# The gating stage of a PEER feed-forward block: distances by TensorE from bf16 digits, digit products by GpSimd, every fourth one-hot by VectorE, and the end of the routing moved into the down pass

## The chip, the cores and the metric

The kernel runs on one core of one Trainium2 chip. The metric is the device time of one execution in microseconds (us), here the median of three runs. One execution is profiled as well; its span and its own time are given below.

## What is computed

The reference is two blocks in sequence, on 256 tokens of 1024 values (16 meta tokens are put ahead of them). The first has a state-space mixer with a convolution branch and a PEER feed-forward; the second has two layers with attention and two SwiGLU feed-forwards each. Only the PEER part matters here:

```python
v1, i1 = lax.top_k(s1, 16); v2, i2 = lax.top_k(s2, 16)      # 8 heads, 128 keys in each half
cand = v1[..., :, None] + v2[..., None, :]
cand_idx = i1[..., :, None] * 128 + i2[..., None, :]
top_s, pos = lax.top_k(cand, 16); expert_idx = take(cand_idx, pos)
gate = jax.nn.softmax(top_s, axis=-1)
act = gelu(einsum("td,thkd->thk", xb, w_down[ib])) * gb
y = einsum("thk,thkd->td", act, w_up[ib])
```

So each token has 128 slots (8 heads by 16), each slot an expert of 16384 (its first key, 0 to 127, and its second key, 0 to 127) and a gate.

## The kernel before, in words

The kernel gathers nothing. The **down pass** computes the hidden value of all 16384 experts for all 256 tokens: 128 units of weights (one unit is 128x1024 values, 512 KB, and makes the hidden values of the 128 experts of one first key, one row of `hid`), each loaded by SyncE into one of 4 slots of `ring`, split by ScalarE (`w_hi`, L415) and VectorE (`ring_lo`, L421) into two fp32r parts, and multiplied by TensorE in 24 matmuls of 256 columns (L526 to L528). ScalarE then applies Gelu from one of PSUM's banks 0 to 3 into `hid` (L2037). `loop_8` is TensorE's side of it, `hidden` ScalarE's, the `low("down", ...)` calls VectorE's. ScalarE and VectorE work two units ahead of TensorE.

Beside the first three quarters of the down pass VectorE does the top-k. Its last part is short: softmax over the slots (ScalarE's Exp at L2043, which in this kernel stands after unit 112, `SAFE` = 28 turns of 4 units; VectorE's sum, reciprocal and product, L1530 to L1532, after the pass), and a split of the second key into a low digit (its value modulo 8, `exp_low`) and a high one (`exp_high`, a multiple of 8).

The **routing's end** comes after the down pass. TensorE transposes first keys, high digits, gates and low digits (L796, banks 4 and 5), so that slots lie on the partitions and tokens along the free axis. VectorE copies three of them to `slot_t` (L1535, L1536), and makes the table `gate_low` in banks 0 to 3 (L1540, L1542; 256 tokens by 8: the gate where the low digit matches, else 0) and the table `high_digit` for 128 tokens by 16 (L1546; 1 where the high digit matches), which it makes again for the second 128 tokens.

The **gating** turns slots into a dense gate per expert and token. It goes in 32 groups n of 8 tokens, with two buffers of each kind. For each group:
- GpSimd writes `diff`, index minus first key, 128x1024 (L2315);
- ScalarE makes of it the one-hot `hots` (`hot_a` in the code): Abs (L2058), then Relu of 1 minus that (L2060), the second in place;
- VectorE writes the digit product `hot_keys` (`hot_b`): high digit by low digit and gate, 128x1024 (L1558);
- TensorE multiplies the two, token by token: 8 fp32 matmuls of 128x128 by 128 columns (L806), which the trace shows as 16 instructions each of weight load and matmul, into banks 4 and 5 or 6 and 7;
- VectorE multiplies the result into `hid` (`big` in the trace, L1565).

The order on each engine is that of its instructions; the semaphores `gates_mm`, `hot_abs`, `hot_diff`, `hot_act`, `hot_dve` and `gated_hid` join them. When the last group is done, the **up pass** starts: ScalarE and VectorE split `hid` (L2050, L1585) and the weights, and TensorE multiplies (L827, 12 matmuls of 512 columns in a unit, 128 units). SyncE has loaded its first four units ahead of the gating, then waits for `gates_mm` 32, issues the loads of `h` (L477, L479), and only then goes on with the stream. ScalarE's queue issues the copy of a bias table within the chip's memory (`bias_rows` from `u_table`, L2062), which the second block needs, just ahead of the gating.

## Time and profile before

| | |
|---|---|
| median of 3 runs | 2464.0 us (2463.56 to 2464.43) |
| profiled execution | 2459.27 us, of which the span from the first to the last instruction is 2457.4 us |
| TensorE matmul busy | 2268.8 us, 92% of the span |
| VectorE busy | 1666.1 us, 68% |
| ScalarE busy | 1140.0 us, 46% |
| GpSimd busy | 250.9 us, 10% |
| mean granted TensorE clock | 0.957 of full |

The profile is of one execution. PE is TensorE's matmul, PEld its weight load, which overlaps PE, DVE is VectorE, ACT ScalarE, POOL GpSimd, SP SyncE; a small q behind a name is that engine's sequencer. Times count from the first instruction. A row names the line, the tiles written and read, the shape, and the number of instructions; what stands in brackets is the engine's idle time before, with what ended it. A matmul's own duration (for 128 columns some 0.27) has its way through the array in it: matmuls follow each other faster than that, so their pace is read from a count over a stretch.

### The profile page before, as it was taken

How to read it: one execution, taken by the hardware profiler on the slowest of the kernel's cores; microseconds unless marked ns; L12 is line 12 of the kernel's file. 1: busy time of each engine (PE TensorE's matmuls, PEld its weight loads, DVE VectorE, ACT ScalarE, POOL GpSimd, SP SyncE). 2: the span in 40 equal slices, each digit the busy share in tenths (PEclk: the TensorE clock that was granted, in tenths of full speed). 3: DMA queues.
4: the chain of work that ended last, by engine and by line, in shares of the span. 5: the costliest groups of instructions: out<-in, count | busy, mean ns of one | idle time of the engine just before them, and what ended most of it. 6: DMA issues, size and time to landing. Idle time of an engine off the chain costs nothing.

```text
span 2457.4 us, 43049 instructions
## 1 busy us (share of the span) xinstructions
PE 2268.8 (92%) x15536; PEld 2077.4 (85%) x15536; DVE 1666.1 (68%) x2997; ACT 1140.0 (46%) x1615; POOL 250.9 (10%) x159
## 2 busy tenths in 40 slices
PE   6988899999988999999799997699999999679999
PEld 5987799999977788888799986499999996457999
DVE  6799569989759655555776644377667665844774
ACT  4432247777768555555444433343444342233443
POOL 4751100000017100000210100010010010001000
PEclk8998999999989999999899997699999998989999
DMA  4432455665560466666555541055555562202655
GB/s 135 148 98 85 129 164 183 185 187 182 186 207 0 143 188 188 188 188 190 171 171 177 175 128 43 9 162 171 175 185 172 170 195 71 69 1 86 188 180 180
DMA packets 107969, 359.47 MB, mean 146 GB/s; under 512 B 12992, under 2 KB 21568, under 8 KB 107760
## 3 DMA queue, kind: packets, MB, share of 16 engines
q1 hardware_dynamic: 105792, 354.04, 46.8%
q10 hardware_dynamic: 2096, 4.36, 0.5%
q8 instruction: 50, 0.82, 0.1%
q14 instruction: 31, 0.25, 0.0%
HBM read 356.22 MB, written 6.46 MB: 148 GB/s over the span
## 4 chain that ended last, share of the span: by engine, by line
PE 81%; DVE 12%; ACT 3%; issue 2%; DMA 1%; POOL 1%; DVEq 0%; SPq 0%; POOLq 0%; ACTq 0%
PE ps L526 19%; PE ps L528 18%; PE ps L527 18%; PE ps L827 14%; DVE ps L1321 2%; DVE hot_keys L1558 1%; PE ps L1134 1%; PE ps L752 1%; PE ps L513 1%; DVE big L1836 1%; ACT w_hi L415 1%; ACT big L2147 1%; DVE ring_lo L421 1%; PE ps L806 1%; PE ps L1073 1%
## 5 line engine op out<-in xcount | busy, mean ns | idle before, releaser
L526 PE MATMUL ps<-hw_hi,w_hi 128*128 128x272 f32 (+1 forms) x3104 | 898.9, 290 | 32.6 <-DVE hw_lo L1197 11.3
L528 PE MATMUL ps<-hw_hi,ring_lo 128*128 128x272 f32 (+1 forms) x3104 | 892.1, 287 | 0.0
L527 PE MATMUL ps<-hw_lo,w_hi 128*128 128x272 f32 (+1 forms) x3104 | 892.0, 287 | 0.0
L421 DVE TENSOR_TENSOR ring_lo<-ring,w_hi 128x1024 fp32r<-128x1024 f32 x580 | 721.1, 1244 | 238.0 <-ACT w_hi L415 234.6
L415 ACT ACTIVATE w_hi<-ring 128x1024 fp32r<-128x1024 f32 x620 | 654.5, 1057 | 462.7 <-DMA ring<-in_ffn_in_dram 166.7
L526 PEld LDWEIGHTS ps<-hw_hi,w_hi 128*128 128x128 f32 x3104 | 593.6, 191 | 48.9 <-issue 29.5
L528 PEld LDWEIGHTS ps<-hw_hi,ring_lo 128*128 128x128 f32 x3104 | 593.5, 191 | 0.0
L527 PEld LDWEIGHTS ps<-hw_lo,w_hi 128*128 128x128 f32 x3104 | 591.9, 191 | 0.3
L827 PE MATMUL ps<-w_hi,hid_parts 128*128 128x512 f32 x1024 | 279.7, 395 | 2.3 <-DVE hid_parts L1585 2.3
L827 PEld LDWEIGHTS ps<-w_hi,hid_parts 128*128 128x128 f32 x1024 | 192.9, 188 | 47.4 <-issue 2.5
L526 PE MATMUL ps<-gated_hi,w_hi 128*128 128x272 f32 (+1 forms) x704 | 201.7, 287 | 3.6 <-DVE big L1628 3.6
L528 PE MATMUL ps<-gated_hi,ring_lo 128*128 128x272 f32 (+1 forms) x704 | 201.2, 286 | 0.0
L527 PE MATMUL ps<-gated_lo,w_hi 128*128 128x272 f32 (+1 forms) x704 | 200.8, 285 | 0.0
L2307 POOL TENSOR_TENSOR sq<-sq 128x272 f32<-128x272 f32 (+1 forms) x49 | 54.0, 1101 | 1397.3 <-ACT sq L1911 697.8
L827 PE MATMUL ps<-ring_lo,hid_parts 128*128 128x512 f32 x512 | 160.5, 395 | 0.0
L1628 DVE TENSOR_TENSOR big<-ps,rstd 128x272 f32<-128x272 f32 (+1 forms) x176 | 76.9, 437 | 116.2 <-PE ps L528 111.1
L526 PEld LDWEIGHTS ps<-gated_hi,w_hi 128*128 128x128 f32 x704 | 132.4, 188 | 4.5 <-issue 4.5
L527 PEld LDWEIGHTS ps<-gated_lo,w_hi 128*128 128x128 f32 x704 | 132.5, 188 | 0.0
L528 PEld LDWEIGHTS ps<-gated_hi,ring_lo 128*128 128x128 f32 x704 | 132.3, 188 | 0.0
L827 PEld LDWEIGHTS ps<-ring_lo,hid_parts 128*128 128x128 f32 x512 | 96.5, 188 | 22.5
L2050 ACT ACTIVATE hid_parts<-big 128x256 fp32r (+1 forms) x128 | 53.4, 418 | 130.1 <-PE ps L827 126.5
L2315 POOL TENSOR_TENSOR diff<-con,slot_t 128x1024 f32<-128x1024 f32 x32 | 64.6, 2022 | 441.1 <-DVE slot_t L1536 420.0
(383 smaller groups left out, 2504.2 us busy)
## 6 DMA issues: line engine op xcount, KB each, us to landing
ring<-in_ffn_in_dram SPq DMA_DIRECT2D x176, 512.0 KB, 3.5
ring<-in_down_dram SPq DMA_DIRECT2D x128, 512.0 KB, 3.5
ring<-in_up_dram SPq DMA_DIRECT2D x128, 512.0 KB, 3.5
ring<-in_ffn_out_dram SPq DMA_DIRECT2D x96, 512.0 KB, 3.5
ring<-in_a_in_dram SPq DMA_DIRECT2D x24, 512.0 KB, 3.5
ring<-in_xbc_dram SPq DMA_DIRECT2D x16, 512.0 KB, 3.6
ring<-in_conf_dram SPq DMA_DIRECT2D x16, 512.0 KB, 3.4
ring<-in_mix_out_dram SPq DMA_DIRECT2D x16, 512.0 KB, 3.5
```

The source lines that it names most:

```text
L415: nc.scalar.activation(w_hi[:, u % RING, :], ring[:, u % RING, :], ACT.Copy).then_inc(hi_done, 1)
L421: eng.tensor_tensor(ring_lo[:, u % RING, :], ring[:, u % RING, :], w_hi[:, u % RING, :].bitcast(F32), ALU.subtract).then_inc(split_done, 1)
L513: last = nc.tensor.matmul(bank_out, ring[:, s, k * P:(k + 1) * P], rhs(k0 + k), start=start and k == 0, stop=stop and k == KD - 1)
L526: nc.tensor.matmul(bank_out, w_hi[:, b, w], hi(k0 + k), start=start and k == 0, stop=False)
L527: nc.tensor.matmul(bank_out, w_hi[:, b, w], lo(k0 + k), start=False, stop=False)
L528: last = nc.tensor.matmul(bank_out, ring_lo[:, b, w], hi(k0 + k), start=False, stop=stop and k == m - 1)
L827: last = nc.tensor.matmul(ps[:, 2 * t + half, :], hid_parts[:, part, t * P:(t + 1) * P], weight[:, s, half * 512:(half + 1) * 512], start= ...
L1321: relay(V_.scalar_tensor_tensor(sums[k % 2], x, V("conf_w", j * CONF_TAPS + k), sums[k % 2], ALU.mult, ALU.add), k == CONF_TAPS - 1)
L1628: V_.tensor_tensor((up_a, up_b)[s % 2][:, p, c0:T], ps[:, s, 0:T - c0], rstd[:, c0:T], ALU.mult).then_inc(acc_free, 1)
L2050: A_(hid_parts[:, c % PARTS, :], at(hid, it * 4 + c), ACT.Copy).then_inc(hid_hi_done, 1)
L2307: nc.gpsimd.tensor_tensor(sq[:, 0, c0:T], sq[:, 0, c0:T], sq[:, k, c0:T], ALU.add).then_inc(sq_sum, 1)
L2315: nc.gpsimd.tensor_tensor(diff[:, b, :, :], bc(C("iota"), 1, 8), bc(keys, 2, P), ALU.subtract).then_inc(hot_diff, 1)
```

## The change

Six things are changed, all in the gating and just ahead of it.
1. **Distances.** TensorE makes the distances that GpSimd made, key minus index, from bf16: a new `distances` issues four matmuls of 512 columns for a group, into banks 0 and 1 or 2 and 3. Two read `keys_bf` (first keys in bf16, tokens on the partitions) against columns of a bf16 identity, each repeated 128 times by a zero step; two subtract the index from one row. ScalarE's Abs now reads PSUM.
2. **Digit products.** GpSimd makes `hot_b` from `high_digit` and a copy of the low table in SBUF (`low_gate`); VectorE did it.
3. **One-hots.** Of every four groups ScalarE makes three; VectorE makes the fourth (n = 3, 7, ...) in one instruction, distance equal to 0.
4. **Routing's end.** The softmax's end, the transposes (six; low digits now stay among the three transposed values and first keys need none), the copies to `slot_t` and the low-digit table (in four quarters of 64 tokens, banks 4 to 7) are inside the down pass, around its turn 28 of 32. The Exp stands one turn earlier (27).
5. After the down pass ScalarE copies the four quarters of the low table to SBUF (one, then the first one-hot, then three), VectorE makes the high table in halves of 64 tokens, and renews a half within the gating after groups 8 and 16. The gating is no loop any more, so nothing is started anew in its middle.
6. ScalarE issues the copy of the bias table after its last one-hot, not before the gating.

Some semaphores are merged (`pool_made`, `dt_sums`, `dt_mm`, `mean_mm`); they count the same events as before. The core of the diff:

```diff
@@ -136,10 +136,11 @@
         with nc.sbuf_tensor("router", [P, KD * T], F32) as router:
             pass
         with nc.sbuf_tensor("hot_keys_2", [P, 2, 8, P], F32) as hot_b:
-            pass
+            with nc.sbuf_tensor("keys_bf", [P, 2, P], BF16) as keys_bf:
+                pass
         h = sb("h", [P, KD, T])
         with nc.sbuf_tensor("high_digit", [P, P, 16], F32) as high_digit:
-            with nc.sbuf_tensor("diff", [P, 2, 8, P], F32) as diff:
+            with nc.sbuf_tensor("low_gate", [P, SEQ, 8], F32) as low_gate:
                 pass
         hw_hi = sb("hw_hi", [P, KD, T], F32R)
         hw_lo = sb("hw_lo", [P, KD, T], F32R)
@@ -168,6 +169,8 @@
         def V(name, j=0, rows=P):
             return vec[0:rows, VEC[name] + j:VEC[name] + j + 1]
         eps = {EPS_1: con[:, CON["eps"]:CON["eps"] + 1], EPS_2: con[:, CON["eps"] + 1:CON["eps"] + 2]}
+
+        TURN_AT = 28
 
         class Carve:
 
...
+        iota_bf, minus_bf = sel_bf[0:1, 0:P], sel_bf[0:1, P:2 * P]
...
-            loop_8("down", normed(META), SEQ)
-
-            pe.wait_ge(route_done, 1)
-            for i, v in enumerate((exp_1, exp_high, gate, exp_low)):
+            loop_8("down", normed(META), SEQ, last=TURN_AT)
+            pe.wait_ge(gate_in, 2)
+            for i, v in enumerate((exp_low, exp_high, gate)):
                 for t in range(2):
                     dst = ps[:, 4 + (2 * i + t) // 4, ((2 * i + t) % 4) * P:((2 * i + t) % 4 + 1) * P]
                     last = nc.tensor.transpose(dst, v[:, t, :], ident)
             last.then_inc(route_turned, 1)
-
-
-            def gates(n, b, first):
-                pe.wait_ge(hot_dve, n + 1)
-                pe.wait_ge(hot_act, n + 1)
-                if not first:
+            loop_8("down", normed(META), SEQ, first=TURN_AT)
+
+            def distances(n):
+
+                if n >= 6 and (n - 2) % 4 == 3:
+                    pe.wait_ge(hot_equal, (n - 2) // 4 + 1)
+                elif n >= 2:
+                    pe.wait_ge(hot_abs, n - 2 - (n - 2) // 4 + 1)
+                tile, tok = n // 16, n % 16 * 8
+                for half in range(2):
+                    dst = ps[:, 2 * (n % 2) + half, :].rearrange("p (t i) -> p t i", i=P)
+                    at0 = tok + 4 * half
+                    nc.tensor.matmul(dst, keys_bf[:, tile, :], bc(ident_bf[:, at0:at0 + 4], 2, P), start=True, stop=False)
+                    last = nc.tensor.matmul(dst, minus_bf, bc(iota_bf, 1, 4), start=False, stop=True)
+                last.then_inc(hot_diff, 1)
+
+            def gates(n):
+                b = n % 2
+                pe.wait_ge(hot_keys_made, n + 1)
+                if n % 4 == 3:
+                    pe.wait_ge(hot_equal, n // 4 + 1)
+                else:
+                    pe.wait_ge(hot_act, n - n // 4 + 1)
+                if n >= 2:
                     pe.wait_ge(gated_hid, n - 1)
+                else:
+                    pe.wait_ge(low_copied, 4)
                 for i in range(8):
                     last = nc.tensor.matmul(ps[:, 4 + 2 * b + i // 4, (i % 4) * P:(i % 4 + 1) * P], hot_b[:, b, i, :],
                                             hot_a[:, b, i, :], start=True, stop=True)
                 last.then_inc(gates_mm, 1)
 
-            gates(0, 0, True)
-            gates(1, 1, True)
-            with pe.Fori(1, SEQ // 16) as it:
-                gates(it * 2, 0, False)
-                gates(it * 2 + 1, 1, False)
+            pe.wait_ge(acc_free, OUT0["up"])
+            pe.wait_ge(pool_made, 3)
+            distances(0)
+            distances(1)
+            for n in range(SEQ // 8):
+                gates(n)
+                if n + 2 < SEQ // 8:
+                    distances(n + 2)
...
-            while ahead[0] % RING != 2:
+            assert ahead[0] <= RING * TURN_AT - 2
+            while ahead[0] < RING * TURN_AT - 2:
                 low("down", ahead[0])
                 ahead[0] += 1
-            with dve.Fori(ahead[0] // RING, UNITS["down"] // RING) as it:
-                for s in range(RING):
-                    low("down", s + 2, it)
             dve.wait_ge(gate_exp, 1)
             sums = gsum.rearrange("p t h -> p (t h)")
             link(V_.tensor_reduce(sums, g3, AX, ALU.add))
             link(V_.reciprocal(sums, sums))
-            V_.tensor_tensor(g3, g3, bc(sums, 2, TOPK), ALU.mult).then_inc(route_done, 1)
+            V_.tensor_tensor(g3, g3, bc(sums, 2, TOPK), ALU.mult).then_inc(gate_in, 1)
+            for s in range(4):
+                low("down", RING * TURN_AT - 2 + s)
             dve.wait_ge(route_turned, 1)
+            V_.tensor_copy(keys_bf[:, :, :], exp_1)
             flat = slot_t.rearrange("p a t -> p (a t)")
             V_.tensor_copy(flat[:, 0:512], ps[:, 4, :])
             V_.tensor_copy(flat[:, 512:768], ps[:, 5, 0:256]).then_inc(slots_ready, 1)
-
-            gate_low = ps[:, 0:4, :].rearrange("p b (t k) -> p (b t) k", k=8)
-            dve.wait_ge(acc_free, OUT0["up"])
-            link(V_.tensor_tensor(gate_low, bc(ps[:, 5, 256:512], 2, 8), bc(C("iota", 8), 1, SEQ), ALU.is_equal))
             dve.wait_ge(slots_ready, 1)
-            V_.tensor_tensor(gate_low, gate_low, bc(slot_t[:, 2, :], 2, 8), ALU.mult).then_inc(low_digit, 1)
-            dve.wait_ge(low_digit, 1)
-
-            def high_digits(tile):
-                link(V_.tensor_tensor(high_digit[:, :, :], bc(slot_t[:, 1, tile * P:(tile + 1) * P], 2, 16),
-                                      bc(C("iota_8", 16), 1, P), ALU.is_equal))
-
+
+            def low_digits(q):
+
+                v = ps[:, 4 + q, :].rearrange("p (t k) -> p t k", k=8)
+                toks = slice(64 * q, 64 * q + 64)
+                link(V_.tensor_tensor(v, bc(slot_t[:, 0, toks], 2, 8), bc(C("iota", 8), 1, 64), ALU.is_equal))
+                V_.tensor_tensor(v, v, bc(slot_t[:, 2, toks], 2, 8), ALU.mult).then_inc(low_digit, 1)
+
+            for q in range(4):
+                low("down", RING * TURN_AT + 2 + q)
+                low_digits(q)
+            with dve.Fori(TURN_AT + 1, UNITS["down"] // RING) as it:
+                for s in range(RING):
+                    low("down", s + 2, it)
+
+            def high_digits(q):
+
+                at_tok = 64 * (q % 2)
+                V_.tensor_tensor(high_digit[:, at_tok:at_tok + 64, :], bc(slot_t[:, 1, 64 * q:64 * q + 64], 2, 16),
+                                 bc(C("iota_8", 16), 1, 64), ALU.is_equal).then_inc(high_ready, 1)
+
+            dve.wait_ge(unit_done, UNIT0["up"])
             high_digits(0)
-
-            def one_hots(n, tile, at_tok, b):
-
-                if not (isinstance(n, int) and n < 2):
-                    dve.wait_ge(gates_mm, n - 1)
-                at_g = at_tok + tile * P
-                high = high_digit[:, at_tok:at_tok + 8, :] if isinstance(n, int) else high_digit[:, bass.ds(at_tok, 8), :]
-                low_g = gate_low[:, at_g:at_g + 8, :] if isinstance(n, int) else gate_low[:, bass.ds(at_g, 8), :]
-                V_.tensor_tensor(hot_b[:, b, :, :].rearrange("p t (a k) -> p t a k", k=8), bc(high, 3, 8), bc(low_g, 2, 16),
-                                 ALU.mult).then_inc(hot_dve, 1)
-
-            def gate_hidden(n, tok, b):
+            high_digits(1)
+
+            def equal_keys(n):
+
+                dve.wait_ge(hot_diff, n + 1)
+                dve.wait_ge(gates_mm, n - 1)
+                b = n % 2
+                V_.tensor_scalar(hot_a[:, b, :, :].rearrange("p i k -> p (i k)"),
+                                 ps[:, 2 * b:2 * b + 2, :].rearrange("p c n -> p (c n)"), 0.0, None, ALU.is_equal).then_inc(hot_equal, 1)
+
+            def gate_hidden(n):
 
                 dve.wait_ge(gates_mm, n + 1)
-                v = hid[:, :, tok:tok + 8] if isinstance(n, int) else hid[:, :, bass.ds(tok, 8)]
+                v = hid[:, :, 8 * n:8 * n + 8]
+                b = n % 2
                 V_.tensor_tensor(v, v, ps[:, 4 + 2 * b:6 + 2 * b, :].rearrange("p c (t i) -> p i (c t)", i=P),
                                  ALU.mult).then_inc(gated_hid, 1)
-            for tile in range(2):
...
+            for n in range(SEQ // 8):
+                gate_hidden(n)
+                if n % 4 == 1:
+                    equal_keys(n + 2)
+                if n in (8, 16):
+                    dve.wait_ge(hot_keys_made, n)
+                    high_digits(n // 8 + 1)
...
             act.wait_ge(s_mm, 8)
-            hidden(0, SAFE)
+            hidden(0, TURN_AT - 1)
             act.wait_ge(gate_in, 1)
             g = gate.rearrange("p t k -> p (t k)")
             A_(g, g, ACT.Exp).then_inc(gate_exp, 1)
-            hidden(SAFE, P // RING)
+            hidden(TURN_AT - 1, P // RING)
 
             def hidden_high(it, c):
 
@@ -2049,23 +2084,32 @@
                     act.wait_ge(unit_done, it * 4 + (UNIT0["up"] + c - 1))
                 A_(hid_parts[:, c % PARTS, :], at(hid, it * 4 + c), ACT.Copy).then_inc(hid_hi_done, 1)
 
-            def hots_act(n, b, first):
-
+            def hots_act(n):
+
+                b = n % 2
                 rows = hot_a[:, b, :, :].rearrange("p i k -> p (i k)")
-                if not first:
+                if n >= 2:
                     act.wait_ge(gates_mm, n - 1)
                 act.wait_ge(hot_diff, n + 1)
-                A_(rows, diff[:, b, :, :].rearrange("p i k -> p (i k)"), ACT.Abs).then_inc(hot_abs, 1)
-                act.wait_ge(hot_abs, n + 1)
+                i = n - n // 4
+                A_(rows, ps[:, 2 * b:2 * b + 2, :].rearrange("p c n -> p (c n)"), ACT.Abs).then_inc(hot_abs, 1)
+                act.wait_ge(hot_abs, i + 1)
                 A_(rows, rows, ACT.Relu, bias=C("ones", 1), scale=-1.0).then_inc(hot_act, 1)
 
+            def copy_low(q):
+
+                act.wait_ge(low_digit, q + 1)
+                A_(low_gate[:, 64 * q:64 * q + 64, :].rearrange("p t k -> p (t k)"), ps[:, 4 + q, :], ACT.Copy).then_inc(low_copied, 1)
+
+            act.wait_ge(unit_done, UNIT0["up"])
+            copy_low(0)
+            hots_act(0)
+            for q in range(1, 4):
+                copy_low(q)
+            for n in range(1, SEQ // 8):
+                if n % 4 < 3:
+                    hots_act(n)
             act.dma_start(bias_rows.rearrange("h (q r) -> h q r", r=REL), bc(u_table, 1, P)).then_inc(u_spread, 16)
-            act.wait_ge(slots_ready, 1)
-            hots_act(0, 0, True)
-            hots_act(1, 1, True)
-            with act.Fori(1, SEQ // 16) as it:
-                hots_act(it * 2, 0, False)
-                hots_act(it * 2 + 1, 1, False)
             act.wait_ge(gated_hid, SEQ // 8)
...
-            def distances(n, tok, b, first):
-                if not first:
-                    pool.wait_ge(hot_abs, n - 1)
-                keys = slot_t[:, 0, tok:tok + 8] if isinstance(tok, int) else slot_t[:, 0, bass.ds(tok, 8)]
-                nc.gpsimd.tensor_tensor(diff[:, b, :, :], bc(C("iota"), 1, 8), bc(keys, 2, P),
-                                        ALU.subtract).then_inc(hot_diff, 1)
-
-            pool.wait_ge(slots_ready, 1)
-            distances(0, 0, 0, True)
-            distances(1, 8, 1, True)
-            with pool.Fori(1, SEQ // 16) as it:
-                distances(it * 2, it * 16, 0, False)
-                distances(it * 2 + 1, it * 16 + 8, 1, False)
+            nc.gpsimd.tensor_copy(iota_bf, C("iota")[0:1, :])
+            nc.gpsimd.memset(minus_bf, -1.0).then_inc(pool_made, 1)
+            for n in range(SEQ // 8):
+                pool.wait_ge(low_copied, n // 8 + 1)
+                pool.wait_ge(high_ready, n // 8 + 1)
+                if n >= 2:
+                    pool.wait_ge(gates_mm, n - 1)
+                at_tok = 8 * (n % 16)
+                nc.gpsimd.tensor_tensor(hot_b[:, n % 2, :, :].rearrange("p t (a k) -> p t a k", k=8),
+                                        bc(high_digit[:, at_tok:at_tok + 8, :], 3, 8), bc(low_gate[:, 8 * n:8 * n + 8, :], 2, 16),
+                                        ALU.mult).then_inc(hot_keys_made, 1)
```

## Rows read from the trace of the kernel before

**Rows 1.** The page: the chain that ended last, by engine, and by line.
```profile
PE 81%; DVE 12%; ACT 3%; issue 2%; DMA 1%; POOL 1%; DVEq 0%; SPq 0%; POOLq 0%; ACTq 0%
```

**Rows 2.** Stretches: length, then each engine's busy time (instructions), clock, DMA share, GB/s.
```profile
core 0: us, PE busy (x) PEld busy (x) DVE busy (x) ACT busy (x) POOL busy (x), PEclk, DMA share, GB/s
672.00:717.00 45.00, 44.74 (x378) 44.54 (x377) 18.61 (x17) 34.28 (x42) 0.00 (x0) 1.00 0.58 179
717.00:730.00 13.00, 2.00 (x16) 1.55 (x14) 11.64 (x10) 4.68 (x5) 8.56 (x4) 0.68 0.89 311
730.00:770.00 40.00, 34.84 (x256) 32.02 (x256) 35.82 (x32) 33.42 (x31) 29.06 (x16) 0.93 0.09 30
840.00:900.00 60.00, 60.00 (x259) 48.62 (x259) 35.88 (x43) 31.55 (x44) 0.00 (x0) 1.00 0.62 191
```

**Rows 3.** Timeline, from the last Gelu of the down pass to the gating's first matmuls.
```profile
718.04 0.38 ACT L2037 ACTIVATE big<-ps 128x256 f32 x1 [1.22 <-PE ps L528]
...
723.60 2.30 DVE L1542 TENSOR_TENSOR ps<-ps,slot_t 128x2048 f32<-128x2048 f32 x1
725.93 3.25 DVE L1546 TENSOR_TENSOR high_digit<-slot_t,con 128x2048 f32<-128x2048 f32 x1
...
730.50 6.15 PE L806 MATMUL ps<-hots,hot_keys 128*128 128x128 f32 x32 [10.20 <-DVE hot_keys L1558]
```

**Rows 4.** Timeline within the gating: two groups, then the last group.
```profile
755.33 1.06 ACT L2058 ACTIVATE hots<-diff 128x1024 f32<-128x1024 f32 x1
755.45 1.21 DVE L1565 TENSOR_TENSOR big<-big,ps 128x1024 f32 x1
...
756.42 1.15 ACT L2060 ACTIVATE hots<-hots,con 128x1024 f32<-128x1024 f32 x1
756.56 1.90 POOL L2315 TENSOR_TENSOR diff<-con,slot_t 128x1024 f32<-128x1024 f32 x1 [0.28 <-ACT hots L2058]
...
764.83 1.21 DVE L1565 TENSOR_TENSOR big<-big,ps 128x1024 f32 x1
...
813.29 1.22 DVE L1565 TENSOR_TENSOR big<-big,ps 128x1024 f32<-128x1024 f32 x1 [0.96 <-PE ps L806]
```

**Rows 5.** Stretches again: the first two groups, and one full group.
```profile
730.40:736.60 6.20, 6.10 (x32) 5.96 (x32) 3.33 (x4) 2.17 (x2) 1.51 (x2) 0.60 0.51 176
755.60:757.50 1.90, 1.83 (x16) 1.84 (x16) 1.90 (x2) 1.87 (x2) 1.62 (x2) 1.00 0.00 0
```

**Rows 6.** Chain of waits at the change of the 128-token half.
```profile
770.45 2.29 DVE high_digit L1546
772.77 1.23 DVE hot_keys L1558
774.12 6.52 PE ps L806 x32
```

**Rows 7.** Groups of instructions: the transposes (chain), bf16 matmuls, ScalarE and VectorE from PSUM.
```profile
719.21 1.11 PE ps L796 x8
...
L1137 PE MATMUL ps<-sel_bf,ident_bf x32: 226/279/434, 2160.4 to 2221.5; 128*128 128x144 bf16 x16, 128*128 128x272 bf16 x16
...
L2030 ACT ACTIVATE big<-ps 128x512 f32<-128x512 f32 x6 | 3.6, 597 | 3.8 <-PE ps L786 3.8
```

**Rows 8.** GpSimd's groups of instructions over the whole span, by form.
```profile
L421 POOL TENSOR_TENSOR ring_lo<-ring,w_hi 128x1024 fp32r<-128x1024 f32 x40 | 96.2, 2416 | 49.6 <-ACT w_hi L415 49.6
L2315 POOL TENSOR_TENSOR diff<-con,slot_t 128x1024 f32<-128x1024 f32 x32 | 64.6, 2022 | 441.1 <-DVE slot_t L1536 420.0 <-ACT hots L2058 21.1
```

**Rows 9.** Timeline of the Exp and of VectorE's three softmax steps.
```profile
673.78 0.42 ACT L2043 ACTIVATE router<-router 128x256 f32<-128x256 f32 x1
...
718.00 0.41 DVE L1530 TENSOR_REDUCE router<-router 128x16 f32<-128x256 f32 x1
...
718.73 0.42 DVE L1532 TENSOR_TENSOR router<-router 128x256 f32<-128x256 f32 x1
```

**Rows 10.** DMA issues (count, KB each, us to landing), and ScalarE at the up pass's fifth unit.
```profile
bias_rows<-u_table ACTq DMA_DIRECT2D x1, 4224.0 KB, 17.7
...
h<-h_spill SPq DMA_DIRECT2D x1, 1024.0 KB, 5.8
...
822.38 1.06 ACT L415 ACTIVATE w_hi<-ring 128x1024 fp32r<-128x1024 f32 x1 [0.44 <-DMA ring<-in_up_dram]
```

72 lines of the change are left out of this document (31 added, 41 removed).

## The prediction

> **What bounds the kernel now.** The chain that ended last is TensorE for 81% of the span and VectorE for 12% [rows 1], so a microsecond counts only where TensorE stands still. I then read stretches around the change [rows 2]. In the down pass TensorE has work all the time at full clock. From 717 to 730 us it works 2.0 of 13 us. In the gating, 730 to 813, it works some 35 of every 40. In the up pass it works all the time again. So this stage has two costs, a head in which TensorE waits for tables, and a loop that VectorE paces.
>
> **The head** is 730.50 less 718.04, 12.5 us from the start of the last Gelu to the first gating matmul, with VectorE making tables [rows 3]. **The loop** runs from 730.50 to the last VectorE product at 813.29 [rows 3, 4]: 82.8 us for 32 groups. Its steady pace is four groups in 764.83 - 755.45 = 9.38 us, 2.35 each [rows 4], which is two VectorE instructions of 1.21 started back to back. At that pace 32 groups are 75 us. The other 8 are the first two groups, 5.96 us of weight loads at a clock of 0.60 where full clock needs 2 x 1.84 [rows 5], and the change of half, where VectorE makes the high table anew and TensorE starts again only at 774.12 [rows 6].
>
> **TensorE's work for a group.** Now it is 16 instructions, 1.83 us in the row [rows 5]; I take 1.82. The change adds four matmuls of 512 columns in bf16. No row has that. Below: in the down pass's form 256 columns follow each other every 45 us / 378 = 0.119, so 512 are 0.24 and without their fixed part not under 0.21 (the clock of 2.4 GHz at a column a cycle). Beside: the up pass's 512 columns take 60 us / 259 = 0.232 [rows 2]. The only bf16 rows have up to 272 columns, duration 0.28, of which 0.16 is the way through the array [rows 7]. I take 0.22, near the upper row less a part of its fp32 weight load: 0.88 a group, with 0.85 to 0.93 as ends, and 1.76 if the zero step of the identity halves the rate. TensorE then has 1.82 + 0.88 = 2.70 us for a group. **That is more than the 2.35 at which the loop runs now**: the change takes VectorE's product away and makes TensorE the bound.
>
> The Trainium skill (TensorE: Matmul & The Clock Gate, Back-to-back issue gap) says that a stream of matmuls with N=512 keeps about 131 ns each, and 216 ns as an isolated gap. By an estimate from the first, the four would be 0.52 us and the group 2.34, no slower than now. This case's fp32r matmuls of 512 columns contradict it with their 232 ns [rows 2]; the gap of 216 agrees with the lower end.
>
> **Do the other engines keep up with 2.70?** VectorE: 1.21 for the product with `hid`, plus a quarter of an equality of 1024 elements from PSUM, 1.2 by the same row: 1.5. ScalarE: Abs and Relu start 1.09 apart and are done in 2.24 [rows 4], for three of four groups: 1.7. From PSUM 512 elements take 0.60 [rows 7], so the Abs stays near 1.06. GpSimd: 1.90 [rows 4], for its other form 2.42 [rows 8]; both are under 2.70. It stands between two TensorE groups: a buffer is free once group n is done and wanted two turns of distances and one group later, 2 x 0.88 + 1.82 = 3.6 us, so 1.90 fits and 2.42 too. The handover distance, Abs, Relu, group, distance has two groups' time: 0.3 + 2.24 + 0.1 + 1.82 + 0.88 = 5.3 against 5.4. It fits, barely, and would pace the loop at 2.67 were TensorE quicker. VectorE's two renewals of the high table, half of 2.28 each [rows 6], lie beside work. They read two SBUF tiles and may hold GpSimd for as long (its distances beside the table at 725.93 and the table itself both stretched, 3.25 for 2.29 [rows 3, 6]), 1.2 us against 1.7 of slack.
>
> The loop after: 32 x 1.82 + 30 x 0.88 = 84.6 us (two distances lie ahead of it). A change of semaphore between every two blocks, 62 of them, costs 0 to 0.06 each; I take 0.03, 1.9 us. The clock: TensorE will have idled some 3.3 us ahead of its first group, and the half clock now costs 5.96 - 3.7 = 2.3 us there [rows 5]; 2.5, ends 0 and 4. Together 89.0, **6.2 more** than 82.8.
>
> **The head after.** Counted from 718.04. The last Gelu ends 718.42; TensorE makes two distances, 1.8 us, from 718.5. ScalarE copies a quarter table by 719.05 (0.60, rows 7), waits for the first distance until 719.6, makes a one-hot by 721.9, and three more copies of 0.60 by 723.7. The first group waits for all four copies, since they read banks 4 to 7. GpSimd's first product waits for the first copy and the first half of the high table (719.3) and is done by 721.3, or 722.4 if the second half holds it. So the first group starts at 723.7, 5.7 us after instead of 12.5, a gain of 6.8. The six transposes go into the down pass, where TensorE is full: 6/8 of 1.11 [rows 7], 0.8 us back. Gain **6.0**.
>
> **What moves into the down pass.** VectorE's three softmax steps take 718.00 to 719.15 now [rows 9]. After the change they stand behind the Exp and ahead of unit 110's low part; that part waits for ScalarE's table load and high part anyway, as at 673.78 now, so they are hidden. The three copies (1.4 us) and the four quarters of the low table (two instructions of a quarter of 2.30 [rows 3], 1.2 us) come with one low part of 1.23 each, 2.4 against the 2.84 of a unit. VectorE works 18.6 of 45 us there [rows 2], and its slack hides them. If the cover were gone it would be all 7 us. I take 0.3, ends 0 and 2. The Exp's pause, TensorE 44.74 of 45 us [rows 2], only moves one turn.
>
> **The moved transfer.** The bias table's copy takes 17.7 us from issue to landing [rows 10], now in the head, at a DMA share of 0.89 [rows 2]. After the change ScalarE issues it after the one-hot of group 30, some 5 us before the last group ends. It then meets the load of `h` (5.8 us, rows 10) and the refills of the ring, behind a share of 0.62 in the up pass [rows 2]. The refill of the fifth unit is issued at 818.77 and ScalarE already waits for it, 0.44 us until 822.38 [rows 10]; TensorE wants that unit at 815.57 + 4 x 2.78 = 826.7, and its split takes until 824.7, so 2 us of delay are free. A refill that lands 2.5 to 4 us late would cost 0.5 to 2. I take 1.0, ends 0 and 5.
>
> **Sum**: +6.2 - 6.0 + 0.3 + 1.0 = +1.5 us. The profiled execution would take 2459.27 + 1.5 = 2460.8; the median of the runs is 4.7 above that execution, so I say 2464.0 + 1.5 = **2465.5 us**. A change of 0.2%, 4.9 us, is what a measurement of this kernel can tell from none. The bounds of the terms put this case at -5 to +9: 2459 to 2473.
>
> **Rivals.**
> - *Faster: bf16 columns are cheaper than fp32r ones.* For it: no row has 512 bf16 columns. Against: 256 and 512 columns of fp32r already run close to a column a cycle. Below 0.82 for the four distances the handover decides; at half the price of the up pass's matmuls, 4 x 0.116 = 0.46, a group takes (0.3 + 2.24 + 0.1 + 1.82 + 0.46) / 2 = 2.46, so the loop is 78.7 + 2.5 = 81.2, 1.6 less than now, and in all -1.6 - 6.0 + 1.3 = -6.3: 2457.7. Chance 0.13. The Trainium skill's 131 ns (TensorE: Matmul & The Clock Gate) is this rival.
> - *Slower: GpSimd's product sets the pace.* It decides from 2.70 us. Its rows are at 1.90 and 2.42 for runs of 128 or more elements [rows 8]; the product walks through runs of 8 with two zero steps, and nothing shows that form on GpSimd. At 3.1 the loop is 99 + 2.5 us, 18.9 more than now, in all +14: 2478. Chance 0.12.
> - *Slower: TensorE reads the repeated identity at half its rate.* 30 x 0.44 for the two of four that read it is +13, 2479; if all four, 2492. Chance 0.07.
> - *Slower: the up pass starves.* Three refills late by 2 to 3 us each, with the rest as forecast: +6 more, 2472. Chance 0.06.
> - *The head stays*: VectorE falls behind in the down pass, and what leaves the head stalls TensorE there: 2470. Chance 0.04.
>
> **How the numbers follow.** The forecast has 0.58: 0.12 of it under -4.9, 0.32 within, 0.14 above. The faster rival gives 0.11 faster and 0.02 same. The slower ones give 0.03 same and 0.26 slower. Sum: faster 0.23, same 0.37, slower 0.40. The range reaches to the faster rival and to GpSimd's, 2456 to 2480, and leaves out the worst of both ends.
>
> **What would show it.** Right: a group of the loop at 2.7 us, with TensorE busy at over 95% from the second group on; distances at 0.88 for four; no TensorE wait for GpSimd; the first group 5.7 us after the last Gelu; clock 0.5 for some 5 us at the loop's start and not in its middle; TensorE in the down pass as full as now. Wrong: distances under 0.8 or over 1.0 a group; GpSimd's product over 2.5; TensorE waiting for Relu in every group; ScalarE waiting over 1 us for refills after the gating.

## The result, and the profile after

The changed kernel takes **2483.68 us** in the median of 4 runs (2483.24 to 2485.12), the kernel before 2464.22 in 4 runs beside it: a ratio of 1.0075 [1.0057, 1.0092]. It is slower by 0.75%; the prediction said 2465.5 us and no more than 2480. In the profiled executions the span went from 2457.4 to 2482.0 us, 24.6 more, and that is the sum to take apart. It is 5 us more than the medians give, because the profiled execution of the kernel before, 2459.27 us, lies that far below its median; the profiled one of the changed kernel, 2483.8, is at its median.

Stretches of the changed kernel (columns as in [rows 2]): the down pass, the head, the gating, the first group, and the 35 us around the start of the up pass.

```profile
672.00:717.00 45.00, 45.00 (x383) 45.00 (x382) 25.53 (x27) 32.55 (x40) 0.00 (x0) 1.00 0.60 180
717.00:730.00 13.00, 9.86 (x58) 7.81 (x57) 4.81 (x4) 8.36 (x12) 4.71 (x2) 0.81 0.32 107
730.00:770.00 40.00, 40.00 (x247) 26.52 (x246) 21.00 (x17) 19.55 (x18) 24.19 (x13) 0.98 0.00 1
727.00:731.00 4.00, 4.00 (x18) 3.38 (x18) 0.34 (x1) 1.78 (x2) 0.42 (x2) 0.50 0.00 0
815.00:850.00 35.00, 27.75 (x142) 21.27 (x141) 15.10 (x17) 13.03 (x17) 6.21 (x4) 0.92 0.64 216
```

Compare with [rows 2]. The down pass stays full of TensorE work. In the gating TensorE is now busy for all of the 40 us where it was for 34.84, and VectorE for 21.00 where it was for 35.82: the bound has moved to TensorE, as forecast. The last row is new. In the 35 us around the start of the up pass TensorE has work for only 27.75; in the same stretch around the old kernel's start (800.64 to 835.64) it has 31.35, and what it lacks there is VectorE's pace in the gating and the 2.3 us at the seam.

Timeline of the changed kernel: the head's two ends, then one full group of the gating, from the end of one block of 16 matmuls to the start of the next.

```profile
721.24 0.38 ACT L2072 ACTIVATE big<-ps 128x256 f32 x1 [1.36 <-PE ps L534]
...
726.87 3.75 PE L832 MATMUL ps<-hots,hot_keys 128*128 128x128 f32 x16 [2.56 <-ACT low_gate L2102]
...
757.56 2.05 PE L832 MATMUL ps<-hots,hot_keys 128*128 128x128 f32 x16
...
759.45 0.38 PE L816 MATMUL ps<-ident_bf,keys_bf 128*128 128x512 bf16 x1
...
759.76 0.09 PEld L817 LDWEIGHTS ps<-sel_bf 1*128 1x128 bf16 x1 [0.32 <-issue]
759.76 0.38 PE L817 MATMUL ps<-sel_bf 1*128 1x512 bf16 x1
...
760.08 0.39 PE L816 MATMUL ps<-ident_bf,keys_bf 128*128 128x512 bf16 x1
...
760.40 0.39 PE L817 MATMUL ps<-sel_bf 1*128 1x512 bf16 x1
760.71 1.86 PEld L832 LDWEIGHTS ps<-hots,hot_keys 128*128 128x128 f32 x16 [0.23 <-issue]
760.72 2.05 PE L832 MATMUL ps<-hots,hot_keys 128*128 128x128 f32 x16
```

The head is 726.87 - 721.24 = 5.63 us where it was 12.46. The group takes 760.72 - 757.56 = 3.16 us (3.15 over many), where 2.70 was forecast. The four distance matmuls start 0.31 to 0.32 us apart, not 0.22. The PEld rows show where the time goes: each weight load starts together with its own matmul, 0.31 us after the matmul ahead, and the load unit idled until then without anybody being waited for ("issue"). A hidden load would have begun with the matmul ahead. Why these loads aren't hidden the experiments below decide.

Groups of instructions of the changed kernel between 715 and 850 us, by form: GpSimd's product, VectorE's product with `hid`, ScalarE's Relu and Abs, VectorE's equality, and its half tables.

```profile
L2363 POOL TENSOR_TENSOR hot_keys<-high_digit,low_gate 128x1024 f32<-128x1024 f32 x32 | 63.3, 1979 | 457.1 <-DVE high_digit L1586 420.5 <-PE ps L832 36.6
...
L1606 DVE TENSOR_TENSOR big<-big,ps 128x1024 f32<-128x1024 f32 x32 | 39.1, 1221 | 53.0 <-PE ps L832 53.0
L2097 ACT ACTIVATE hots<-hots,con 128x1024 f32<-128x1024 f32 x24 | 27.6, 1149 | 0.8
...
L2095 ACT ACTIVATE hots<-ps 128x1024 f32<-128x1024 f32 x24 | 24.6, 1024 | 46.6 <-PE ps L817 46.6
...
L1598 DVE TENSOR_SCALAR hots<-ps 128x1024 f32<-128x1024 f32 x8 | 9.8, 1225 | 0.0
...
L1586 DVE TENSOR_TENSOR high_digit<-slot_t,con 128x1024 f32<-128x1024 f32 x4 | 6.4, 1628 | 0.0
```

No engine but TensorE is near 3.15 us a group. Within the loop all three wait for it: the releasers of their idle time are its lines (GpSimd's 420.5 us for `high_digit` is its wait ahead of the gating).

At the seam to the up pass: the DMA issues of the changed kernel between 805 and 850 us (count, KB each, median us to landing), and two pieces of its chain of waits.

```profile
bias_rows<-u_table ACTq DMA_DIRECT2D x1, 4224.0 KB, 20.9
ring<-in_up_dram SPq DMA_DIRECT2D x4, 512.0 KB, 6.2
h<-h_spill SPq DMA_DIRECT2D x1, 1024.0 KB, 15.7
```
```profile
829.93 4.60 PE ps L856 x12
...
834.69 10.44 DMA ring<-in_up_dram
```

The load of `h` takes 15.7 us where it took 5.8 [rows 10], the refills 6.2, and for 10.44 us the chain rests on one refill. The chain leaves TensorE after 12 matmuls of the up pass; TensorE itself makes 48, those of the four units loaded ahead, and then stands without work for some 5 us.

The sum of the two profiled executions, stage by stage:

| stage | before | after | difference | forecast |
|---|---|---|---|---|
| start to last Gelu | 718.04 | 721.24 | +3.2 | +1.1 |
| head | 12.5 | 5.6 | -6.8 | -6.8 |
| loop, to VectorE's last product | 82.8 | 100.8 | +18.0 | +6.2 |
| last product to up pass | 2.3 | 2.3 | 0 | 0 |
| up pass | 351.6 | 360.0 | +8.4 | +1.0 |
| the rest | 1290.2 | 1292.1 | +1.9 | 0 |

The forecast's 1.1 in the first row is its 0.8 for the transposes and 0.3 for the moved work. Of the measured 3.2, 2.5 are there before the change's code begins (289.82 for 287.30 at the query units, below). The +1.9 in the last row need not be the change's either: a second profile of the kernel before (below) has 1293.9 there.

### The profile page after: what moved, and what is told of

It reads as the page before. It is cut to its first block, busy times and chain, and to the rows that moved or that the text cites. A ratio compares the mean times of both kernels' runs of the same rounds, so it can differ in the third digit from the quotient of the medians.

```text
span 2482.0 us, 42952 instructions
## 1 busy us (share of the span) xinstructions
PE 2309.5 (93%) x15662; PEld 2088.1 (84%) x15662; DVE 1642.3 (66%) x2982; ACT 1125.1 (45%) x1603; POOL 250.1 (10%) x161
## 4 chain that ended last, share of the span: by engine, by line
PE 84%; DVE 10%; ACT 3%; DMA 1%; issue 1%; POOL 1%; SPq 0%; POOLq 0%; ACTq 0%; DVEq 0%
PE ps L532 19%; PE ps L534 18%; PE ps L533 18%; PE ps L856 14%; PE ps L832 3%; DVE ps L1350 2%; PE ps L1163 1%; PE ps L759 1%; PE ps L519 1%; PE ps L817 1%; PE ps L816 1%; DVE big L1871 1%; ACT big L2191 1%; DVE ring_lo L427 1%; ACT w_hi L421 1%
## 5 line engine op out<-in xcount | busy, mean ns | idle before, releaser
L2363 POOL TENSOR_TENSOR hot_keys<-high_digit,low_gate 128x1024 f32<-128x1024 f32 x32 | 63.3, 1979 | 457.1 <-DVE high_digit L1586 420.5
```

Source lines behind the costliest of these rows:

```text
L2363: nc.gpsimd.tensor_tensor(hot_b[:, n % 2, :, :].rearrange("p t (a k) -> p t a k", k=8), bc(high_digit[:, at_tok:at_tok + 8, :], 3, 8), bc( ...
```

## The experiments

Each set ran beside the kernel before on the same chip; the median of before was 2464.2 to 2465.1. The changed kernel itself ran only in the first set, so a difference against it compares two sets, and 1 us of it can be theirs. Theory A of the loop: a weight load isn't hidden when it has another number of rows than the matmul ahead (128 and 1 here). Theory of the seam: the bias table's copy takes the DMA engines from `h` and the ring.

**The copy back at its old place.**

```
+            act.dma_start(bias_rows..., bc(u_table, 1, P)).then_inc(u_spread, 16)
             act.wait_ge(unit_done, UNIT0["up"])
             copy_low(0)
...
-            act.dma_start(bias_rows..., bc(u_table, 1, P)).then_inc(u_spread, 16)
```

> The changed kernel with one edit: ScalarE issues the copy of the bias table ahead of the gating again, as before the change. Theory (the copy, issued late, takes the DMA engines from the refills of the ring at the start of the up pass): from the first to the last matmul of the up pass goes from 360.0 us back to about 352, TensorE waits under 1 us for hidden parts after its fourth unit, and the kernel takes about 8 us less, 2475 to 2477. Rival (the up pass loses its time to the clock or to the load of h, which waits for the gating in both kernels): the same 360 us, the kernel within 1 us of the changed one.

Measured 2475.88 us, ratio 1.0044 [1.003, 1.0058], 7.8 less than the changed kernel. DMA issues of this kernel between 805 and 850 us, and its chain of waits:

```profile
ring<-in_up_dram SPq DMA_DIRECT2D x6, 512.0 KB, 3.5
h<-h_spill SPq DMA_DIRECT2D x1, 1024.0 KB, 5.7
```
```profile
831.10 353.17 PE ps L856 x1512
```

The transfers at the seam are back to their old durations, and the chain runs through the up pass on TensorE alone, 1512 matmuls in one piece. It takes 353.2 us instead of 360.0: the copy alone makes 6.8 of the up pass's 8.4 us. Some 5 of them are the stop itself. The rest follows from it: behind the stop the granted clock is at half again, 0.72 in the mean of the first 6 us, and TensorE makes 19 matmuls there where at full clock it makes 26.

```profile
847.86:853.86 6.00, 6.00 (x19) 4.82 (x20) 2.98 (x4) 2.12 (x3) 0.00 (x0) 0.72 0.04 11
```

**The second term with 128 rows.** The same sum is computed: the one row of -1 becomes 128 rows of -1/128, against 128 rows of the digit's number.

```
-        iota_bf, minus_bf = sel_bf[0:1, 0:P], sel_bf[0:1, P:2 * P]
+        iota_bf, minus_bf = sel_bf[:, 0:P], sel_bf[:, P:2 * P]
...
-            nc.gpsimd.tensor_copy(iota_bf, C("iota")[0:1, :])
-            nc.gpsimd.memset(minus_bf, -1.0).then_inc(pool_made, 1)
+            nc.gpsimd.tensor_copy(iota_bf, C("iota"))
+            nc.gpsimd.memset(minus_bf, -1.0 / P).then_inc(pool_made, 1)
```

> The changed kernel with the subtracting matmul on 128 partitions: weights -1/128 and the index on every partition, instead of -1 and the index on one. Same columns, same type, same zero steps. Theory A (TensorE does not load weights under a running matmul when the number of rows changes, 128 to 1 and back, so each of the four distance matmuls waits 0.1 us for its weights): the four follow each other every 0.22 instead of 0.32 us, a group takes 2.72 to 2.80 instead of 3.15, the loop is 12 to 13 us shorter and the kernel 12 us faster. Theory B (a bf16 weight load never lies under a bf16 matmul of 512 columns): no change, 0.32 and 3.15. Theory C (the repeated columns are read at two thirds of the rate): no change either, with the weight load as early as in the other matmuls.

Measured 2468.28 us, ratio 1.0016 [1.0007, 1.0025], 15.4 less than the changed kernel. Timeline of a group in this kernel, TensorE's loads and then its matmuls:

```profile
771.79 0.10 PEld L817 LDWEIGHTS ps<-sel_bf 128*128 128x128 bf16 x1
772.01 0.10 PEld L816 LDWEIGHTS ps<-ident_bf,keys_bf 128*128 128x128 bf16 x1
```
```profile
770.01 1.95 PE L832 MATMUL ps<-hots,hot_keys 128*128 128x128 f32 x16
771.79 0.38 PE L816 MATMUL ps<-ident_bf,keys_bf 128*128 128x512 bf16 x1
772.01 0.38 PE L817 MATMUL ps<-sel_bf 128*128 128x512 bf16 x1
772.22 0.38 PE L816 MATMUL ps<-ident_bf,keys_bf 128*128 128x512 bf16 x1
772.44 0.38 PE L817 MATMUL ps<-sel_bf 128*128 128x512 bf16 x1
772.65 0.61 PE L832 MATMUL ps<-hots,hot_keys 128*128 128x128 f32 x4
```

The load of each weight now begins with the matmul ahead (771.79 under 771.79), the matmuls start 0.216 apart, and the group takes 2.64 us: 1.78 for the 16 and 0.86 for the four. That is more than theory A had promised (2.72 to 2.80, and 12 us for the kernel), because the block of 16 got shorter too (1.78 for 1.89). Line 816 reads the identity with a zero step in both kernels and runs at the full rate, and nothing about bf16 is dear. Only the row count changed, and theory A holds for 1 and 128 rows. Whether the number of rows itself counts, or which part of the array they fill, no run here separates.

**Half as many changes of row count.** The four matmuls in the order keys, keys, minus, minus, so that two of four changes in a group fall away.

```
                 for half in range(2):
                     ...
                     nc.tensor.matmul(dst[half], keys_bf[:, tile, :], bc(ident_bf[:, at0:at0 + 4], 2, P), ...)
+                for half in range(2):
                     last = nc.tensor.matmul(dst[half], minus_bf, bc(iota_bf, 1, 4), ...)
```

> The changed kernel with the four distance matmuls of a group in another order: the two with the keys as weights first, then the two with the row of -1. Nothing else. Theory A (the load waits where the number of rows changes): two of the four changes go, a group takes 3.15 - 2 x 0.1 = 2.95 us and the kernel 6 to 7 us less. Theories B and C: no change.

Measured 2478.82 us, ratio 1.0053 [1.0039, 1.0067], 4.9 less than the changed kernel. Timeline of a group, TensorE's matmuls:

```profile
770.15 2.05 PE L833 MATMUL ps<-hots,hot_keys 128*128 128x128 f32 x16
772.04 0.60 PE L816 MATMUL ps<-ident_bf,keys_bf 128*128 128x512 bf16 x2
772.57 0.60 PE L818 MATMUL ps<-sel_bf 1*128 1x512 bf16 x2
773.10 0.38 PE L833 MATMUL ps<-hots,hot_keys 128*128 128x128 f32 x1
```

The group takes 2.95 us: 1.89 and twice 0.53. That splits the 0.51 us which the changed kernel's 3.15 stands above 2.64. Two matmuls with the same row count take 0.43, with one change among them 0.53, so a change costs 0.10, four of them 0.41. The other 0.11 lies in the block of 16, which takes 1.89 behind a matmul with one row and 1.78 behind one with 128. Both changed kernels have it once, so this experiment takes away 0.20 a group, and 30 x 0.20 = 6. In the profiles the stretch from the first block of 16 to the last VectorE product is 6.4 us shorter (94.4 for 100.8); the medians show 4.9.

**The routing's end alone.** Of the whole change only this stays: routing's end and the low-digit table in the down pass, the high table made by quarters, and the loop written out. GpSimd makes distances and VectorE the product again, the bias table's copy stands ahead, the low table lies in banks 4 to 7 and the gates in 0 to 3, and the transposed low digits are kept in the idle tile `std`.

```
+            loop_8("down", normed(META), SEQ, last=TURN_AT)
+            pe.wait_ge(gate_in, 2)
+            ...
+            loop_8("down", normed(META), SEQ, first=TURN_AT)
...
+            V_.tensor_copy(std[:, 0:SEQ], ps[:, 5, 256:512]).then_inc(slots_ready, 1)
...
             for n in range(SEQ // 8):
                 gate_hidden(n)
                 if n + 2 < SEQ // 8:
                     one_hots(n + 2)
+                if n in (6, 14):
+                    dve.wait_ge(hot_keys_made, n + 2)
+                    high_digits((n + 2) // 8 + 1)
```

> Only the part of the change that moves the routing's end and the low-digit table into the down pass (with eight transposes, and the low digits kept in a spare tile), the high table in halves of 64 tokens and the loop unrolled; distances by GpSimd, products and hidden values by VectorE, all one-hots by ScalarE as before the change, with the low table in PSUM banks 4 to 7 and the gates in 0 to 3, and the bias table's copy ahead of the gating. Theory (the head and the break at the half are worth having, and only the new division of the work among the engines loses): the first group starts 5 us after the last Gelu instead of 12.5, the steady pace is 2.35 us a group, the break at the half is gone, and the kernel is 8 to 11 us faster than the one before, 2453 to 2456. Rival (the pace of 2.35 cannot be held with short high-digit renewals that keep GpSimd's port, or the moved steps stall the down pass): within 3 us of the one before.

Measured **2453.25 us**, ratio 0.9954 [0.994, 0.9968]: faster than both kernels. Timeline of its head, then of VectorE late in its loop, then of a quarter table in the loop:

```profile
720.78 0.38 ACT L2051 ACTIVATE big<-ps 128x256 f32 x1 [1.06 <-PE ps L534]
720.90 2.92 DVE L1561 TENSOR_TENSOR high_digit<-slot_t,con 128x1024 f32<-128x1024 f32 x1
...
725.17 1.19 PE L813 MATMUL ps<-hots,hot_keys 128*128 128x128 f32 x4 [4.53 <-DVE hot_keys L1573]
```
```profile
794.05 1.21 DVE L1582 TENSOR_TENSOR big<-big,ps 128x1024 f32<-128x1024 f32 x1
795.18 1.21 DVE L1573 TENSOR_TENSOR hot_keys<-high_digit,ps 128x1024 f32<-128x1024 f32 x1
796.31 1.21 DVE L1582 TENSOR_TENSOR big<-big,ps 128x1024 f32<-128x1024 f32 x1
```
```profile
745.10 1.81 DVE L1561 TENSOR_TENSOR high_digit<-slot_t,con 128x1024 f32<-128x1024 f32 x1
...
749.34 1.83 PE L813 MATMUL ps<-hots,hot_keys 128*128 128x128 f32 x14 [2.06 <-DVE hot_keys L1573]
```

The head is 4.4 us, shorter than in the changed kernel, since VectorE goes from the first half table straight to the first product. VectorE still paces the loop, at 1.13 a step and 2.26 a group where [rows 4] show 2.35. The two stops for the high table remain: at 745.10 and 765.05 a quarter table of 1.81 us stands in VectorE's row, and the block of 16 behind it starts 4.11 us after the one ahead. Together they cost 3.7 us; the kernel before has one stop in which 6.90 us pass between two blocks, with the granted clock at 0.50 from 773 to 779 us. So the break at the half isn't gone, as the expectation had it, but it is cheaper. From the first matmul to the up pass's first are 805.33 - 725.17 = 80.2 us, where before were 815.57 - 730.50 = 85.1.

**Both repairs** (the copy ahead and the 128 rows), and then **ScalarE for all one-hots** (both repairs, and VectorE's `equal_keys` left out, so that `hots_act` makes all 32; TensorE's waits follow).

```
                 gate_hidden(n)
-                if n % 4 == 1:
-                    equal_keys(n + 2)
...
-                if n % 4 < 3:
-                    hots_act(n)
+                hots_act(n)
```

> The changed kernel with both edits together: the bias table's copy ahead of the gating, and the subtracting matmul on 128 partitions. Theory (the two losses are separate, and what is left is TensorE's own work for a group, 1.78 for the gates and 0.86 for the distances, against 2.35 before): 7 to 8 us for the one and 13 to 15 for the other come off the changed kernel, 2460 to 2463, a little faster than the kernel before, by the head, and 7 to 10 us slower than the kernel with only the routing's end moved. Rival (the division of work is as good as the old one once the two faults are gone): 2453 or less.

> The kernel with both edits, and ScalarE makes all 32 one-hots; VectorE's equality of every fourth group is left away. Theory (TensorE's 2.64 us for a group is the bound, ScalarE's two passes take 2.2, and the handover distance, Abs, Relu, group takes two groups' time or just less): the pace goes from 2.64 to at most 2.70 a group, the kernel is 0 to 2 us slower than with the fourth one-hots on VectorE. Rival (ScalarE paces the loop or the handover does, and the fourth one-hot is needed): 2.8 or more a group, 5 us or more slower.

Measured 2459.09, ratio 0.9979 [0.997, 0.9988], and 2459.73, ratio 0.9984 [0.9975, 0.9993]. Two blocks of 16 in the timeline of the second:

```profile
771.53 1.95 PE L827 MATMUL ps<-hots,hot_keys 128*128 128x128 f32 x16
...
774.18 0.50 PE L827 MATMUL ps<-hots,hot_keys 128*128 128x128 f32 x3
```

The blocks start 774.18 - 771.53 = 2.65 us apart here, and 773.30 - 770.65, as much, in the kernel with both repairs: TensorE's sum, whoever makes the fourth one-hot. With both repairs the kernel is a little faster than expected (2460 to 2463), and ScalarE alone costs 0.6 us, within the expected 0 to 2. The two repairs add up, and a little more (7.8 and 15.4 alone, 24.6 together, all against the changed kernel's median): with the 128 rows alone the late copy does more harm than before, the profiled up pass being 1.4 us longer than the changed kernel's (366.9 for 365.5, first to last matmul). But even repaired, TensorE's 2.65 us is more than VectorE's 2.26, and the whole idea stays some 6 us behind the routing's end alone (7 to 10 were expected).

**The 2.5 us ahead of the change.** The query units' first DMA in the chain of waits starts at 287.30 us before and at 289.82 after, though the code up to there differs only in shared semaphores. The kernel before was run again; then it was run with the merged semaphores, and the routing's end alone with the mixer's old ones (`dt_done`, `dt_turned`, `dt_copied`, `var_mm`); GpSimd's merged `pool_made` stays in that last kernel.

```
-            last.then_inc(dt_turned, 1)
+            last.then_inc(dt_mm, 1)
```

> The kernel before, unchanged, for a second profile of it. In the changed kernel's profile 2.5 us were already lost at the start of the query units, long ahead of the change (289.8 against 287.3 us). Theory (that is the difference of one execution from another): this profile has the query units' start anywhere between 287 and 290. Rival (the merged semaphores in the mixer cost it): 287.3 again, within 0.3.

> The kernel before with only the merged semaphores of the mixer and of GpSimd (dt_sums, dt_mm, mean_mm, pool_made); no instruction moved. The kernels made from the changed one start the query units 1.7 to 3.1 us later than the kernel before in both its profiles (287.3). Theory (the merged counts themselves cost it): the query units start at 289 or later and the kernel takes 2 us more. Rival (it hangs on how the program as a whole is laid out or fetched): 287.3 within 0.5, the same time as before within 1 us.

> The kernel with only the routing's end moved, with the semaphores of the mixer as before the change. Theory (merged counts cost 2 us): 2451, with the query units at 287.3. Rival (layout): 2453 to 2454 again, with them at 288 to 290.

Measured 2465.61, ratio 1.0008 [0.9998, 1.0018]; 2464.6, ratio 0.9997 [0.9988, 1.0007]; 2455.25, ratio 0.9956 [0.9943, 0.997]. The chain of waits of the last two, in this order (the kernel before has this piece at 287.29, as in its first profile):

```profile
290.13 4.15 DMA ring<-in_query_dram
```
```profile
290.30 4.44 DMA ring<-in_query_dram
```

The second profile of the kernel before repeats 287.29, which speaks against a mere difference between executions, though it is only two. With the merged semaphores the shift is 2.8 us, and yet the median is the same; the profiled execution doesn't get it back (2466.05 us, where the second one of the kernel before took 2462.92). With the mixer's old semaphores the routing's end alone is as late as with the merged ones and gains the same 0.45%, so those four by themselves aren't the cause. `pool_made` could be: all kernels that start late share it, and it was never split by itself. The shift is there long before the query units, since the mixer's output matmuls begin at 215.0 and 214.9 in the two profiles before, at 217.2 in the changed kernel and at 217.7 with the merged semaphores. The medians show no cost of the merged semaphores (2464.6 beside 2465.14); what causes the shift stays open.

This shift isn't why the stage table adds up to 24.7 while the medians differ by 19.5. The second profile of the kernel before reaches the up pass at the same time as the first (815.57 there) and goes through it in the same time:

```profile
815.54 351.62 PE ps L827 x1512
```

Its execution took 3.7 us longer (2462.92 for 2459.27), and all of it lies behind the up pass, 1293.9 us for 1290.2. The table's first column is of an execution that was quick there.

## Why the prediction was wrong

**The bound: right.** The forecast was that TensorE takes over from VectorE, and that this costs more than the removed VectorE product brings. The row of 40 busy us in 40 shows it, and so does the experiment with ScalarE making all one-hots: with less work on VectorE the pace stays at TensorE's 2.65. One reading was loose: the old pace of 2.35 isn't two instructions of 1.21 back to back. In the timeline they start 1.13 apart, and one step in four takes 1.28; the written-out loop has 1.13 throughout.

**The head: right.** Forecast 5.7 us, measured 5.63, with the wait for the last ScalarE copy of the low table named in the row.

**The price of a distance matmul: the step that failed.** It was put at 0.22 us "less a part of its fp32 weight load", that is, with a bf16 load hidden under the matmul ahead. With equal rows that is exact (0.216 measured). But two of the four have one row and two have 128, and no load is hidden across such a change. A group costs 3.15 us where the forecast had 2.70 and 0.06 for the two changes of semaphore: 30 x 0.39 = 11.7 us, which is the loop's whole miss (100.8 for 89.0). With the loads hidden it comes in under the forecast: 84.9 us in the kernel with both repairs, from its first block at 726.64 to 811.57. So the changes of row count cost 15.9 us, and 4.1 of them were covered by terms put too high, among them 1.9 for changes of semaphore, of which nothing shows. The forecast had allowed for a change of semaphore between blocks, and never asked what a change of shape costs. Rows of the trace before could have warned, in the timeline of another stage:

```profile
2185.77 0.19 PEld L1161 LDWEIGHTS ps<-big 16*64 16x64 f32 x2 [0.34 <-issue]
2186.34 0.19 PEld L1162 LDWEIGHTS ps<-big 128*64 128x64 f32 x2 [0.39 <-issue]
```

The load of 16 rows begins 0.21 us after the matmul ahead of it (128 rows, 2185.56), and the load of 128 rows behind it 0.30 us after the matmul ahead (16 rows, 2186.04), while the neighbours with equal rows begin with theirs. The second is the cleaner sign: the first load carries a wait for a semaphore, and type and column count change there as well.

The Trainium skill (TensorE: Matmul & The Clock Gate, Back-to-back issue gap) was weighed in the prediction, and the 216 ns of its isolated gap hold here for bf16 with equal rows, also in a stream (0.216 us measured); its 131 ns for a stream do not.

**The moved transfer: right in mechanism, wrong in size.** The term was 1.0 us with ends at 0 and 5; the experiment that moves it back gives 7.8 us in the medians and 6.8 in the up pass's length. The forecast counted with refills 2.5 to 4 us late behind 2 us of slack. It looked at each transfer's own duration and not at the queue. SP issues the load of `h` at 827.65 and the next refill at 834.69, both on one queue; beside the copy the load takes 15.7 us, until 843.4. The refill's first packets (4 KB each) start at 840.8, when those of `h` and of the meta rows thin out (the last of them start at 843), and it lands at 845.1, having held the chain for 10.44 us where the same refill took 3.6 before. The rival "the up pass starves" came near in size, 6 us on top of the term, but not in its account, which had three refills late by 2 to 3 us each and not one late by 7 behind `h`; its chance of 0.06 was too small for a copy of 4.2 MB set between a 1 MB load and a full stream.

**The clock: right, and one more.** The first block of 16 takes 3.75 us with a granted clock of 0.50, which is the level of 1.2 GHz, and with the distances behind it the first group takes 5.47 us where the later ones take 3.15: 2.3 more, where 2.5 was forecast. Not foreseen was the up pass's start: in its first 6 us the copy-ahead kernel has a clock of 0.72 and makes 19 matmuls, the kernel before 1.00 and 26.

```profile
831.10:837.10 6.00, 6.00 (x19) 4.86 (x20) 1.84 (x3) 1.92 (x3) 0.00 (x0) 0.72 0.71 186
```
```profile
815.57:821.57 6.00, 6.00 (x26) 4.90 (x27) 3.06 (x4) 2.07 (x4) 0.00 (x0) 1.00 0.83 250
```

Seven matmuls of 0.232 [rows 2] are 1.6 us, all that the up pass still loses with the copy ahead (353.2 against 351.6).

**The rivals that fell.** GpSimd's product took 1.98 us with runs of 8 and zero steps, not over 2.5. The repeated identity is read at full rate. ScalarE's one-hots never held a group (no wait of TensorE's for them in the loop). The down pass took in the routing's end at 0.7 us (3.2 less the 2.5 ahead of it). The faster rival, cheap bf16 columns, fell too: 0.216 is what they take.

**The range** ended at 2480 and should have reached further: 2465.5 with either miss alone, 11.7 us in the loop or 7 at the seam, lies inside it, and with both, 2484.2, it does not.

## What to carry to other kernels

Work taken from the pacing engine is paid on the one that receives it: 0.86 us of TensorE for 1.21 us of VectorE looks like a gain until the engines' sums per turn are set side by side (2.65 against 2.26 to 2.35); the prediction did that, and was right in it. Keep the row counts of neighbouring matmuls equal, by padding with 1/128 where need be, or put those with equal rows together. A large transfer doesn't belong where a stream of refills starts; and of a change with several parts each should be tried alone, since here one part by itself is 0.46% faster and the rest took that and more. Two profiles of one kernel are worth having before a stage table is read to the microsecond: here they differ by 3.7 us in a stage that nobody touched.

## What the runs showed of the hardware

- A weight load with another number of rows than the matmul ahead (128 to 1, 1 to 128) waits for the end of its columns: 0.10 us for each at full clock (0.316 us a matmul for 0.216), and 0.11 more in a block of fp32 matmuls behind a one-row matmul.
- A moving operand with a zero step and runs of one element (the repeated identity) streams 512 columns in 0.216 us, the same as one with runs of 128 (the repeated index).
- Where VectorE reads two SBUF tiles beside GpSimd, either can stretch. In the changed kernel two quarters of the high table take 2.36 us at 721.14, and one takes 2.03 at 757.63 beside GpSimd's product; in the kernel with the routing's end alone the first takes 2.92. In that kernel with the mixer's old semaphores the same table takes 1.22, and GpSimd's instruction beside it 2.96 instead of 1.90. GpSimd's first two products, beside the table, take 4.71 where two later ones take 3.91. The Trainium skill (GPSIMD Engine Reference, Specifications) says that GpSimd's SBUF interfaces are shared with VectorE, with contention for VectorE instructions with two SBUF inputs; the trace agrees with those numbers. VectorE's products that read one tile and PSUM keep 1.22 us beside GpSimd.
- The granted clock of the up pass's first 6 us is 0.72 in six profiles (the changed kernel, the copy ahead, the keys and minus in pairs, both repairs, the routing's end alone in either form) and 1.00 in five (the kernel before twice and with merged semaphores, the 128 rows, ScalarE for all one-hots), after the same 2.3 us of TensorE standing still. It isn't whether the loop ahead was full of TensorE work: the routing's end alone has gaps like the kernel before, and both repairs and ScalarE for all one-hots have full loops and differ. What decides is open and wasn't tried.
